# Attention of a hybrid decoder step: TensorE's order of values, turned result and scores

## The reference

```python
att = jnp.einsum('bqgrd,bqkgd->bqgrk', qg, k_sel.astype(f32)) * (ATT_HEAD_DIM ** -0.5)
att = jnp.where(valid[:, :, None, None, :], att, -jnp.inf)
p = jax.nn.softmax(att, axis=-1)
o = jnp.einsum('bqgrk,bqkgd->bqgrd', p, v_sel.astype(f32))
```

## Time and profile before

| what | value |
|---|---|
| median of 3 runs | 2813.6 us (2808.52 to 2816.48) |
| the profiled execution | 2809.43 us |
| its span, from the first to the last instruction | 2807.7 us |
| TensorE busy | 2656.1 us (95% of the span) |
| GpSimd busy | 1189.0 us (42%) |
| VectorE busy | 1097.1 us (39%) |
| ScalarE busy | 567.1 us (20%) |
| mean granted clock of TensorE | 0.951 |
| bytes moved by the DMAs | 188.45 MB, 67 GB/s on average |

### The profile page before, as it was taken

How to read it: one execution, slowest core, us unless ns; L and a number is a source line. 1 busy time by engine, 2 the same in 40 slices (tenths; PEclk the granted TensorE clock), 3 DMA queues, 4 the chain that set the end, 5 groups by cost and what they waited for, 6 DMA issues and landing times. The chain is left out here.

```text
span 2807.7 us, 43411 instructions
## 1 busy us (share of the span) xinstructions
PE 2656.1 (95%) x16469; PEld 2540.1 (90%) x16469; DVE 1097.1 (39%) x2395; ACT 567.1 (20%) x1011; POOL 1189.0 (42%) x1520
## 2 busy tenths in 40 slices
PE   7999879999999999999878998999999999999998
PEld 7899758999999999999747997788999999999998
DVE  6959365342112121123258974655332121121223
ACT  3010143221010010111034533444121010010112
POOL 5534303555455555556302411000655455554552
PEclk8999978999999999999879986999999999999998
DMA  6534443311111111111212224202111111111111
GB/s 200 107 79 95 113 136 94 110 38 45 48 49 46 45 45 45 47 51 42 89 29 83 85 74 143 84 16 76 45 38 48 50 45 45 45 45 49 48 45 68
DMA packets 291412, 188.45 MB, mean 67 GB/s; under 512 B 41030, under 2 KB 281290, under 8 KB 290522
## 3 DMA queue, kind: packets, MB, share of 16 engines
q1 hardware_dynamic: 271350, 179.85, 21.3%
q10 hardware_dynamic: 19940, 7.01, 2.1%
HBM read 151.84 MB, written 34.98 MB: 67 GB/s over the span
## 5 line engine op out<-in xcount | busy, mean ns | idle before, releaser
L403 POOL TENSOR_TENSOR w_hi<-w_raw,ones 128x256 fp32r<-128x256 f32 x720 | 620.0, 892 | 1321.9 <-PE ps L414 1194.6
L406 POOL TENSOR_TENSOR w_lo<-w_raw,w_hi 128x256 fp32r<-128x256 f32 x720 | 527.7, 764 | 25.6
L414 PE MATMUL ps<-next_hi,w_hi 128*128 128x344 f32 x1920 | 417.9, 327 | 13.5 <-PEq L1902 9.0
L414 PE MATMUL ps<-out_x_hi,w_hi 128*128 128x344 f32 x1920 | 408.5, 321 | 6.9 <-DVE out_x_lo L1939 6.9
L414 PE MATMUL ps<-next_lo,w_hi 128*128 128x344 f32 x1920 | 412.9, 324 | 0.0
L414 PE MATMUL ps<-next_hi,w_lo 128*128 128x344 f32 x1920 | 410.5, 323 | 0.0
L414 PE MATMUL ps<-out_x_lo,w_hi 128*128 128x344 f32 x1920 | 408.2, 321 | 0.0
L414 PE MATMUL ps<-out_x_hi,w_lo 128*128 128x344 f32 x1920 | 406.3, 320 | 0.0
L1964 DVE TENSOR_TENSOR resid<-ps,resid 128x344 f32 (+1 forms) x240 | 108.9, 509 | 705.3 <-PE ps L414 705.3
L414 PEld LDWEIGHTS ps<-next_hi,w_hi 128*128 128x128 f32 x1920 | 327.2, 191 | 15.2 <-issue 14.3
L414 PEld LDWEIGHTS ps<-out_x_hi,w_hi 128*128 128x128 f32 x1920 | 324.1, 188 | 7.3 <-issue 7.3
(11 more groups left out here) (551 smaller groups left out, 2783.7 us busy)
## 6 DMA issues: line engine op xcount, KB each, us to landing
w_raw<-in_w_up SPq DMA_DIRECT2D x64, 512.0 KB, 4.1
w_raw<-in_w_down SPq DMA_DIRECT2D x64, 512.0 KB, 4.0
w_raw<-in_w_in SPq DMA_DIRECT2D x36, 512.0 KB, 4.4
resid_spill<-resid SPq DMA_DIRECT2D x2, 4128.0 KB, 13.7
ml_inputs<-in_ring SPq DMA_DIRECT2D x16, 516.0 KB, 2.8
resid<-resid_spill SPq DMA_DIRECT2D x4, 2064.0 KB, 7.7
w_raw<-in_w_out SPq DMA_DIRECT2D x16, 512.0 KB, 4.2
keys<-in_cache_k SPq DMA_DIRECT2D x64, 128.0 KB, 2.0
```

The costliest lines, as they stand in the source:

```text
L403: m.nc.gpsimd.tensor_tensor(parts(hi[:, k]), x[:, k], one, ALU.mult)
L406: last = m.nc.gpsimd.tensor_tensor(parts(lo[:, k]), x[:, k], hi[:, k], ALU.subtract)
L414: ins = nc.tensor.matmul(out[c], parts(w), parts(x[:, token_cols(c)]), start=first and n == 0, stop=last and n == 2)
```

## The change

In each turn of TensorE's loop `scores(n + 2)` moves from behind `turn_probs(n)` to the end of the turn, behind `values(n - 1)` and `turn(n - 2)`. Nothing else is edited; the lists of the other engines stay as they are.

```diff
             for n in range(n_heads + 2):
                 if n < n_heads:
                     turn_probs(n)
-                if n + 2 < n_heads:
-                    scores(n + 2)
                 if 0 <= n - 1 < n_heads:
                     values(n - 1)
                 if n >= 2:
                     turn(n - 2)
+                if n + 2 < n_heads:
+                    scores(n + 2)
```

## The result

The changed kernel takes 2935.27 us (median of 4 runs, 2934.1 to 2939.17) against 2811.06 us before: 1.0441 times as long, 95% interval [1.0426, 1.0455], 124 us more. The forecast was 2926 us, 112 us more.

The account below looks back on a forecast made before the run. TensorE, busy 205.09 of 212 us in layer 1's attention, was taken as the bound; 78.5 us of waits, 22.3 of clock falls and 11.4 of late rise made 112 us on 2813.6: 2926 us, range 2884 to 2968.

Parts of the forecast that it names:

- The chain: Attention: values(n) wait for mask(n+2), then norm(n-1), after the scores; 1.89 us, with 0.49 us of transposes to run under.
- The step: Wait at TensorE's values: 1.40 us a head, 61 times; 1.48 us in the last block.
- The sum of 78.5 us: Attention: 61 waits of 1.40 us, 85.4 us, less the 6.9 us TensorE had free.
- The two terms: Attention clock: 14 falls behind samples' tasks at 1.59 us, 22.3 us; second block staying at 1.2 GHz, 11.4 us.
- Rival 1: Attention: the clock holds and only the waits cost, 2892 us; chance 0.20.
- Rival 2: Attention: the clock stays at 1.2 GHz for the whole stage after missing its rise, 3052 us; chance 0.05.
- rival 3: Attention: not slower, values come earlier and free norm earlier, giving back at most 6.9 us, 2807 us; chance 0.04.
- The other waits keep their cover: Attention: exponentials, copies of probs_t and turn's wait for norm(n-2) stay covered, adding no wait.

Follow-up runs that it names:

- run 1: Changed kernel with VectorE's norm(n-1) put ahead of mask(n+2), TensorE keeping the new order: 2852.85 us, 1.015 times the kernel before.
- run 2: Changed kernel with VectorE's norm(n-1) ahead of mask(n+2) and ScalarE's out(n-2) ahead of exps(n+2): 2818.38 us, 1.0013 times the kernel before.
- run 7: Changed kernel with a useless VectorE write of 128x768 values between mask(n+2) and norm(n-1), in 62 heads: 3006.04 us, 1.0714 times the kernel before.
- 8: Kernel before with a useless VectorE write of 128x768 values between mask and norm: 2824.4 us, 1.0045 times the kernel before.
- run 10: Changed kernel with TensorE uselessly computing the first 512 columns of scores(n+2) between turn_probs(n) and values(n-1): 2906.01 us, 1.0326 times the kernel before.
- run 3: Changed kernel with only ScalarE's out(n-2) put ahead of exps(n+2): 2938.64 us, 1.0442 times the kernel before.
- run 9: Changed kernel with the sixteen samples' tasks issued behind the matmuls of their values instead of ahead: 2920.89 us, 1.039 times the kernel before.

## Why the prediction was right

- **The chain.** `values` wait for a norm queued behind the mask of scores that now come last: shown by 1 and 2, which take the queueing away and leave TensorE's order, and by 7 and 8, where the same write costs 71 us behind the change and 11 without it.
- **Its size.** The step gave 1.48 us for the last block; 1.48 was measured. The sum of 78.5 us stands against 70.6 us more free time on TensorE, plus the part of each wait that the modelled ends cover (0.16 us, 61 times, 10 us): 80.
- **The clock.** The two terms, 22.3 + 11.4 = 33.7 us, stand against the rest of the attention's growth, 119 - 80 = 39 us; run 10 shows that some 23 us of it are the clock. The rise came late as assumed, in the eighth head of the second block, and the falls were 13 against 14, all behind tasks. What was too small is the price of a fall. From head 16 on, turn against turn of the kernel before (by the starts of L3037), a turn grew by about 1.50 us where no fall was near, and all of them together by 96.2 us: 96.2 - 47 x 1.50 = 26 us more, by this estimate 2.0 us for each of 13 falls and not 1.59, as some last over more than one head. The forecast's shortfall, 112 us against 124, is 7 us in the attention and the scatter ahead of it.
- **The ground for the falls.** The price and the cause were taken from one fall in the indexer's stage, behind sixteen sparse loads. Sixteen of the same loads stood 6 us earlier, as the row below shows, and the clock stayed at 1.00 (1608 to 1617). So the rows did not show that such loads always bring a fall; a fall at each task was a guess, and it came out in 13 of 15.

  ```profile
  1609.76 1.95 PE L2711 MATMUL ps<-small,keys 128*128 128x4 f32 x16
  ```

- **The skill's rule against it.** By the Trainium skill ("TensorE: Matmul & The Clock Gate", section "Why this matters for your kernels") waits as short as these would leave the clock alone. Rival 1, which would be its outcome, stood at 2892 us. The trace agrees for the heads without a task: there waits of up to 1.6 us brought no fall once the clock had risen. It differs where a task follows the wait, and in run 7, where waits of some 2 us brought falls by themselves; over the attention the clock went from 0.96 to 0.83. So the measurement decides against the rule as the whole story. Rival 2 (low for the whole stage) and rival 3 (not slower) did not come.
- **What it missed.** "The other waits keep their cover" was not true of `turn`'s wait for `out(n-3)`, and the prediction did not look at it. On ScalarE that copy stands behind the exponentials of the late scores. In the changed kernel VectorE's wait hides it (run 3), so no number was hurt; with VectorE's queue put right the kernel is still 42 us slower (run 1), and putting ScalarE's right as well leaves some 4 (run 2).

## What to carry to other kernels

When a producer is moved later in one engine's list, look at the lists of its consumers: whatever stands behind the waiting instruction there is late too, and somebody may be waiting for that. Here a step that changed no instruction and no wait cost 4%, and moving two finished steps ahead of the waiting ones on the other engines gave all but some 4 us of it back. And a wait on TensorE can cost more than its length, as here, where the granted clock fell with it.

## What the runs showed that was not expected

- The clock of a stage can be worth useless work: 61 pieces of 0.86 us more on TensorE, inside its waits, made the kernel 29 us faster (run 10).
- The two queues' waits overlap and don't add: each half of the move alone costs 114 and 48 us, both 124; freeing the one that ends first gives nothing (run 3).
- A sample's task, sixteen weight loads with four-column matmuls, had a fall of the clock behind it in 13 of 15 cases where it followed a wait (1.00 ahead of 2019, 0.50 from 2020 on), and in none of the heads from 42 on where dense work stood on both sides (1.00 from 1926 to 2062 in run 9). In shorter heads of run 9 it fell there too.
